# Turning a key page before, not after, the page ahead of it is scored, in the paged attention of a hybrid decoder step

## The reference

```python
def step(carry, pages):
    o_acc, sv = carry
    kp = cache_k[pages]
    vp = cache_v[pages].astype(jnp.float32)
    zp = jnp.einsum('bqhd,bkhd->bhqk', q, kp).astype(jnp.float32) * SB_SCALE + bh
    lmp = jax.nn.log_sigmoid(-zp)
    rcp = lax.cumsum(lmp, axis=3, reverse=True)
    wp = jnp.exp(jax.nn.log_sigmoid(zp) + rcp - lmp + sv[..., None])
    o_acc = o_acc + jnp.einsum('bhqk,bkhd->bqhd', wp, vp)
    return (o_acc, sv + rcp[..., 0]), None
```

## Time and profile before

| | us |
|---|---|
| median of 3 runs | 3016.62 (3013.79 to 3017.61) |
| the profiled execution, whole | 3015.11 |
| its span | 3013.3 |
| PE busy | 2880.0 (96% of the span) |
| ACT busy | 1216.5 (40%) |
| DVE busy | 1764.5 (59%) |
| waits of PE on the copies of key pages, 670 to 980 us | 6.0 in 6 waits |

### The profile page before, as it was taken

How to read it: one execution, slowest core, us unless ns; L and a number is a source line. 1 busy time by engine, 2 the same in 40 slices (tenths; PEclk the granted TensorE clock), 3 DMA queues, 4 the chain that set the end, 5 groups by cost and what they waited for, 6 DMA issues and landing times.

```text
span 3013.3 us, 60900 instructions
## 1 busy us (share of the span) xinstructions
PE 2880.0 (96%) x24110; PEld 2726.0 (90%) x24110; DVE 1764.5 (59%) x2738; ACT 1216.5 (40%) x1481; POOL 293.6 (10%) x545
## 2 busy tenths in 40 slices
PE   6799999879999999969999999999999999999999
PEld 2499999868888899869999999999999999999999
DVE  0433343344444432398888888888888755555553
ACT  1345555444444421254444444444444422222222
POOL 0000000011212100011111111111111100000000
PEclk9799999989999999979999999999999999999999
DMA  9966555455766697523333333333333633333323
GB/s 336 338 168 171 162 162 141 141 160 177 228 201 212 191 250 220 143 69 111 103 112 104 113 109 97 111 109 111 111 95 114 206 108 108 103 106 107 105 81 107
DMA packets 608837, 444.53 MB, mean 148 GB/s; under 512 B 14553, under 2 KB 556111, under 8 KB 607453
## 3 DMA queue, kind: packets, MB, share of 16 engines
q1 hardware_dynamic: 584630, 353.39, 40.2%
q0 software_dynamic: 23904, 84.15, 8.9%
q10 hardware_dynamic: 144, 4.72, 0.4%
HBM read 408.14 MB, written 34.06 MB: 147 GB/s over the span
## 4 chain that ended last, share of the span: by engine, by line
PE 86%; DVE 5%; ACT 4%; DMA 3%; issue 1%; SPq 0%; POOL 0%; ACTq 0%; DVEq 0%; POOLq 0%
PE ps L713 40%; PE ps L1113 35%; PE ps L729 2%; DMA wide<-in_w_ada_dram 2%; PE ps L911 1%; PE ps L926 1%; PE ps L791 1%; DMA ada_o<-in_w_ada_dram 1%; PE ps L809 1%; PE ps L737 1%; PE ps L959 1%; PE ps L763 1%; PE ps L843 1%; PE ps L915 1%; ACT w_hi L1218 1%
## 5 line engine op out<-in xcount | busy, mean ns | idle before, releaser
L1113 PE MATMUL ps<-ops,w_hi 128*128 128x288 f32 x4608 | 920.4, 296 | 1.5 <-DVE w_lo L2076 1.5
L1113 PEld LDWEIGHTS ps<-ops,w_hi 128*128 128x128 f32 x4608 | 742.0, 189 | 1.7 <-DVE w_lo L2076 1.7
L1113 PE MATMUL ps<-ops,w_lo 128*128 128x288 f32 x2304 | 679.5, 295 | 0.0
L1692 DVE TENSOR_TENSOR w_lo<-raw,w_hi 128x1024 fp32r<-128x1024 f32 x240 | 294.0, 1225 | 647.6 <-ACT w_hi L1218 646.5
L713 PE MATMUL ps<-gs,w_hi 128*128 128x288 f32 x3072 | 534.0, 296 | 0.0
L1218 ACT ACTIVATE w_hi<-raw 128x1024 fp32r<-128x1024 f32 x240 | 253.6, 1057 | 679.1 <-PE ps L713 649.9
L713 PEld LDWEIGHTS ps<-gs,w_hi 128*128 128x128 f32 x3072 | 452.4, 189 | 0.0
L1113 PEld LDWEIGHTS ps<-ops,w_lo 128*128 128x128 f32 x2304 | 437.9, 190 | 0.0
L713 PE MATMUL ps<-act_hi,w_hi 128*128 128x288 f32 x1792 | 403.4, 307 | 18.4 <-DVE act_lo L1756 13.5
L713 PE MATMUL ps<-act_hi,w_lo 128*128 128x288 f32 x1792 | 385.1, 297 | 0.0
L713 PE MATMUL ps<-act_lo,w_hi 128*128 128x288 f32 x1792 | 384.7, 297 | 0.0
(11 more groups left out here) (353 smaller groups left out, 3218.4 us busy)
## 6 DMA issues: line engine op xcount, KB each, us to landing
raw<-in_w_up_dram SPq DMA_DIRECT2D x120, 512.0 KB, 4.3
raw<-in_w_down_dram SPq DMA_DIRECT2D x128, 384.0 KB, 3.3
raw<-in_w_in_dram SPq DMA_DIRECT2D x80, 512.0 KB, 4.5
ada_q<-in_w_ada_dram SPq DMA_DIRECT2D x80, 512.0 KB, 5.4
wide<-in_w_ada_dram SPq DMA_DIRECT2D x32, 1024.0 KB, 11.2
page<-in_cache_k_dram POOLq DMA_DIRECT2D x64, 512.0 KB, 4.6
page<-in_cache_v_dram POOLq DMA_DIRECT2D x64, 512.0 KB, 4.5
ada_o<-in_w_ada_dram SPq DMA_DIRECT2D x48, 512.0 KB, 6.5
```

The lines of the kernel that those rows point to most:

```text
L1113: mm = pe.matmul(ps[:, bank, 0:HALF], w[slot][:, kk, :], moving(i, kk, low), start=i not in ADDED and kk == 0 and w is w_hi and not low, s ...
L1692: dve.tensor_tensor(w_lo[s][:], raw[s][:], w_hi[s][:].bitcast(F32), ALU.subtract).then_inc(lo_done, 1)
```

## The change

At a point with a key page the order of the two calls on PE is turned round from block 1 on: the page is transposed first, and the page ahead of it is scored behind that. In block 0 this was the order already. Nothing else is touched: no other engine's program, no semaphore, no buffer.

```diff
@@ -978,10 +978,8 @@
                 if (i, p) in LAST_KEYS:
                     score(LAST_KEYS[i, p])
                 if k is not None:
-                    if i and k not in (32, 48):
-                        score(k - 1)
                     turn_keys(i, p, k)
-                    if not i and k:
+                    if k not in (0, 32, 48):
                         score(k - 1)
                 if v is not None:
                     weigh_page(i, p, v)
```

## The result

The changed kernel takes 3020.76 us (median of 20 runs, 3014.44 to 3025.08) against 3015.14 us before (20 runs, 3008.36 to 3019.12): ratio 1.0020, 95% interval 1.0013 to 1.0027. It is slower by 5.6 us (3.9 to 8.1 by the interval), at the edge of what was called no change. The forecast was +4.4 us.

The account below looks back on a forecast made before the run. PE was taken to bound the kernel (86% of the span); 1.0 (order on PE) + 2.35 (late copies) + 1.0 (point (1, 0)) = +4.35 us, forecast 3021.0 us on a median of 3016.62, range 3015 to 3026.

Parts of the forecast that it names:

- Part 1: PE's order at 46 key points: 1.81 us a point instead of 1.78, counted at 34 points, +1.0 us.
- Rival A: Slower than 0.2%: the new neighbours on PE cost over 0.06 us a point, up to 0.12 (3025.5 us); chance 0.27.
- Part 2: Page copies wait for the score: ACT's starts 0.33 us later, DVE's 0.10 earlier; chains behind ACT's copy cost +2.35 us.
- 0.23 + 0.33: Block 4: ACT's late copies delay the chain to (4, 5) by 0.23 us and that to (4, 9) by 0.33.
- the gelu's 0.20: Last point of blocks 3 and 5: of ACT's 0.33 us delay, 0.20 reaches the gelu that the first gate product reads.
- the chain to (1, 9): Block 1: ACT's late copy delays the copy of the weights that the first value page waits for, +0.3 us.
- -0.15 for (1, 4): Block 1: PE's wait at (1, 4) hangs on DVE's own chain, which comes earlier, so 0.15 us is gained.
- Part 3: Point (1, 0): page 16's transposes stand ahead of score 15, delaying `z_left` and the gate product behind it, +1.0 us.
- B: Faster than 0.2%: transposes going first fill PE's six waits for a copied page, at most -6.0 us; chance 0.05.
- C: PE's half-speed clock stretches: one may come at (2, 0), 3022.7 us, or the one near 880 us go, 3019.3; chance 0.15.
- D: ACT's delayed copies cost nothing because slack takes them, leaving 3018.6 us; chance 0.13.

Follow-up runs that it names:

- e3: Changed kernel with the old order back at ten points, whose copy or score precedes something PE waits for; timed 1.0008 of the kernel before.
- e2: Kernel before with the new order at point (1, 0) alone; trace only, page 15 to score 63 in 292.70 us (before 293.29).
- e1: Changed kernel with the old order back at point (1, 0) alone; trace only, page 15 to score 63 in 298.58 us (changed kernel 297.90).
- e6: Changed kernel with a second SBUF home for the left half of every second page; median 3011.54 us, 0.9993 of the kernel before.
- e4: Kernel before with the new order at nine points, (1, 0) left old; trace only, page 15 to score 63 in 298.14 us (before 293.29).
- e5: Kernel before, PE's order untouched, ACT's left copy also waiting for the right transposes from block 1 on; timed 1.0022 of the kernel before.
- e8: Kernel before, old order, with a second SBUF home for left halves; trace only, page 15 to score 63 in 290.76 us (before 293.29).

## Why the prediction was right, point by point

- **Part 1, the order on PE.** Forecast 1.81 us a point from borrowed pieces, measured 1.81 (832.24 to 834.05), with L911 0.26 behind the products and L926 0.53 behind L915. The working stopped at the first product, though. Counted to the second pair most turned points cost 0.05, not 0.03 (2.18 against 2.12 at (4, 3)), and the points (3, 9) and (5, 9), which the forecast did not tell apart, give back 0.09 each. That e3 comes out at 1.1 with 0.9 forecast is in part these two errors cancelling. Rival A, up to 0.12 a point, falls. The count of changes of mode by the Trainium skill (TensorEngine Tiling (Array Packing), Key Properties) would have given 0.00, also within what the timing can tell; the rows give 0.03 to the first product.
- **Part 2, the copies.** ACT's start was forecast 0.33 later and came 0.37 later at (4, 3). Block 4: forecast 0.23 + 0.33 and some 0.09 for the order, measured 0.78; block 6 the same. There PE is 0.33 later from the last pair ahead of (6, 3) to the product behind (6, 5), and 0.33 again from the last pair ahead of (6, 6) to the product behind (6, 8), what the order costs on the way included. The sign that I gave, PE's waits at (2, 9), (4, 9) and (6, 9) 0.3 longer, came true at (2, 9) alone (1.61 against 1.33). At (4, 9) and (6, 9) the wait stayed (0.98 against 0.96), and the chain's delay had already been met on the way, most of it at (4, 8) and (6, 8): right size, wrong place. Block 3, with the gelu's 0.20: measured 0.41 against 0.40. Block 2: 0.49 against 0.42. (2, 0): PE waits 2.03 in place of 1.70, as forecast, +0.33.
- **The part that was mis-sized** is block 1. I forecast 0.3 for the chain to (1, 9) and -0.15 for (1, 4). The chain had its size and not its place: it shows at (1, 8), where the transposes of the weights take 1.39 us in place of 1.11, held between their halves by DVE's copy of the page before. At (1, 4) PE still waits 1.00 us (before 1.02); the clock differs just ahead of it, so that the runs don't show whether anything came back there. With what the clock gave back, block 1 and (2, 0) cost some 1.1 us, not the 0.7 that I had added up; the difference is the -0.15 and the order at 0.05 a point.
- **Part 3, point (1, 0).** Forecast 1.0, measured 0.97, alone 1.05 (e2), and gone with the old order there (e1). The gate product does not fall at 677.5 but at 675.44, only because the whole stretch starts 2.0 us earlier in this trace.
- **Sum.** 4.35 forecast for the stretch, 4.61 measured, of it an estimated -0.4 by the clock; timed 5.6. That the whole came out close owes a little to luck: the clock hid part of what block 1 cost. Whether it is "within 0.2%" or "slower" is not decided by the measurement: the interval of the ratio reaches from 1.0013 to 1.0027.
- **Rivals.** B: no wait was covered, there are six as before; e6 shows what it would have taken, a free home, which brings 7.4 us. C: the slow stretches did come and go, near 880 us for 1.6 us and at (2, 0), in e4, for about 1.7, as worked out. D falls with e5.

## What to carry to other kernels

When two steps on the bounding engine are exchanged, ask what each of them releases, and where that engine's follower goes on from there; here 0.03 us a point on average was PE's part, and 0.37 us of delay on an engine that is 40% busy made more than half of the loss. A wait that names one engine (DVE) can be paid by another two steps up the chain (ACT): delay or free that one alone, and see whether the wait moves. An order that lets work be made sooner is worth something only if there is a place to put it: transposes first lost 5.6 us with one home, timed, and with two took 1.9 us less than before (3011.54 against 3013.41), with an interval that still holds no change.

## What the runs showed of the hardware that I had not expected

The slow stretches of PE's clock are not fixed by the program alone: behind a wait of 1.86 us near 880 us the stretch is there in before and after, and in e2 and e8, where PE does the same work in the same order at that place, it is missing, for 1.6 us less. The same 64 matmuls of L952 behind the same wait, in before and in e2:

```profile
879.62 1.90 PE L895 MATMUL ps<-xc,wg 128*128 128x288 f32 x4 [1.86 <-ACT La L1384]
881.45 2.92 PE L952 MATMUL ps<-vs,X 128*32 128x128 f32 x64
```

```profile
878.35 1.24 PE L895 MATMUL ps<-xc,wg 128*128 128x288 f32 x4 [1.86 <-ACT La L1385]
879.52 1.95 PE L952 MATMUL ps<-vs,X 128*32 128x128 f32 x64
```

That is a third of the whole effect studied here, so a sum over the stretch from a single trace can be off by more than a part of the change is worth, while the pieces that no slow stretch touches repeat to 0.01 us where the work is the same. This agrees with the statement of the Trainium skill (TensorE: Matmul & The Clock Gate, What's actually happening) that the gate's watch is free-running.
